# Expert weights in half loads, the residual's buffer lent to one of them, and a regrouped first and last stage

## The reference

```python
x = x + merged @ w_out                                   # x1
h2 = rms_norm(x, norm_ffn)
x = x + moe_ffn(h2, ...)        # 32 experts, each token goes to 2 of them:
#   y = (silu(xb @ w_gate[e]) * (xb @ w_up[e])) @ w_down[e], weighted and added
gate = sigmoid(rms_norm(x, norm_ple) @ w_ple_gate)
x = x + gate * (pemb @ w_ple_proj)                       # pemb: 320 rows of 256
y = rms_norm(x, final_norm)
```

## Time and profile before

| | |
|---|---|
| median of 3 runs | 1094.8 us (1091.55 to 1095.89) |
| the profiled execution | 1092.05 us, its span 1090.4 us |
| PE matmul busy | 1051.1 us (96%) |
| PE weight load busy | 539.3 us (49%) |
| DVE, ACT, POOL busy | 26%, 21%, 9% |
| mean granted TensorE clock | 0.983 |
| chain that ended last: PE, DMA | 50%, 10% |
| expert gate and up loads, issue to landing | 20.6 to 26.0 us (medians) |

### The profile page before, as it was taken

How to read it: one execution, slowest core, us unless ns; L and a number is a source line. 1 busy time by engine, 2 the same in 40 slices (tenths; PEclk the granted TensorE clock), 3 DMA queues, 4 the chain that set the end, 5 groups by cost and what they waited for, 6 DMA issues and landing times.

```text
span 1090.4 us, 14358 instructions
## 1 busy us (share of the span) xinstructions
PE 1051.1 (96%) x5786; PEld 539.3 (49%) x5786; DVE 285.7 (26%) x771; ACT 232.6 (21%) x488; POOL 98.7 (9%) x142
## 2 busy tenths in 40 slices
PE   6999999999999999999989999999999999999994
PEld 3468887555666667775533333333333333333342
DVE  1122011466334324111441111111111111122513
ACT  2012011266322244000221111111111111111333
POOL 0020031000222220000020000000000000001000
PEclk8999999999999999999979999999999999999997
DMA  9972239220545578563349999999999999999801
GB/s 329 263 248 40 78 85 187 78 78 1 165 147 161 176 291 191 222 229 157 113 161 386 426 427 428 426 428 427 427 428 429 428 427 428 425 429 421 266 1 49
DMA packets 57251, 286.32 MB, mean 263 GB/s; under 512 B 10273, under 2 KB 14650, under 8 KB 44844
## 3 DMA queue, kind: packets, MB, share of 16 engines
q1 hardware_dynamic: 47020, 256.99, 60.9%
q0 software_dynamic: 9936, 28.46, 9.0%
q10 hardware_dynamic: 240, 0.09, 0.0%
HBM read 276.57 MB, written 18.25 MB: 270 GB/s over the span
## 4 chain that ended last, share of the span: by engine, by line
PE 50%; DMA 10%; DVE 1%; issue 1%; ACT 0%; POOL 0%; DVEq 0%; SPq 0%; POOLq 0%; ACTq 0%
PE ps L1119 17%; PE ps L554 9%; PE ps L1143 8%; DMA late<-in_w_exp_up_dram 7%; PE ps L1091 4%; PE ps L1014 3%; PE ps L610 3%; DMA late<-y_rows 3%; PE ps L1104 1%; PE ps L1095 1%; PE ps L1133 1%; DMA y_rows<-reg_xh,slot_row 1%; PE ps L991 1%; PE ps L617 1%; PE ps L575 1%
## 5 line engine op out<-in xcount | busy, mean ns | idle before, releaser
L1119 PE MATMUL ps<-ring,reg_xh 128*64 128x512 f32 x512 | 150.4, 602 | 4.2 <-DMA ring<-in_w_exp_up_dram 2.5
L1119 PE MATMUL ps<-late,reg_xh 128*64 128x512 f32 x336 | 150.3, 601 | 2.0 <-DMA reg_k<-in_w_exp_up_dram 1.2
L1119 PEld LDWEIGHTS ps<-ring,reg_xh 128*64 128x64 f32 x512 | 47.1, 138 | 89.2 <-issue 86.5
L1482 ACT ACTIVATE reg_xh<-ps 64x512 f32<-64x512 f32 x32 | 34.0, 1063 | 229.7 <-PE ps L1119 229.7
L2053 DVE TENSOR_TENSOR reg_xh<-reg_xh,ps 64x512 f32<-64x512 f32 x32 | 22.1, 691 | 225.9 <-ACT reg_xh L1482 225.9
L1119 PE MATMUL ps<-reg_k,reg_xh 128*64 128x512 f32 x176 | 79.6, 606 | 0.0
L833 PE MATMUL ps<-reg_xh,ring 128*128 128x320 f32 x256 | 73.5, 436 | 0.0
L1119 PEld LDWEIGHTS ps<-late,reg_xh 128*64 128x64 f32 x336 | 44.7, 138 | 47.4 <-issue 45.9
L1091 PE MATMUL ps<-reg_xh 128*64 128x512 f32 x256 | 62.3, 607 | 1.1 <-DVE reg_xh L1971 1.1
L2257 POOL DMA_INDIRECT y_rows<-reg_xh,slot_row x29 | 28.3, 975 | 382.5 <-ACT reg_xh L1493 342.3
L554 PE MATMUL ps<-reg_xh,ring 128*128 128x320 f32 x224 | 60.9, 433 | 0.0
(11 more groups left out here) (403 smaller groups left out, 1339.4 us busy)
## 6 DMA issues: line engine op xcount, KB each, us to landing
ring<-in_w_exp_gate_dram SPq DMA_DIRECT2D x21, 2048.0 KB, 21.5
ring<-in_w_in_dram SPq DMA_DIRECT2D x13, 2048.0 KB, 11.1
late<-in_w_exp_gate_dram SPq DMA_DIRECT2D x11, 2048.0 KB, 20.6
reg_k<-in_w_exp_up_dram SPq DMA_DIRECT2D x11, 2048.0 KB, 25.0
ring<-in_w_exp_down_dram SPq DMA_DIRECT2D x11, 2048.0 KB, 25.0
ring<-in_w_exp_up_dram SPq DMA_DIRECT2D x11, 2048.0 KB, 26.0
reg_o<-in_w_exp_down_dram SPq DMA_DIRECT2D x11, 2048.0 KB, 26.1
late<-in_w_exp_up_dram SPq DMA_DIRECT2D x10, 2048.0 KB, 25.6
```

The lines of the kernel that those rows point to most:

```text
L1119: last = pe.matmul(out[64 * part:64 * part + 64, :], xb[:, k, :], ws_[part][:, k, :], start=(k == 0), stop=(k == KT - 1))
L1482: act.activation(sg.rearrange("p (m q) -> p q m", m=4), ps[0:64, 2 + par, :].rearrange("p (q m) -> p q m", m=4), ACT.Silu).then_inc(silu_d ...
```

## The change

- First products: the first `w_in` chunk is loaded in two halves (k 0 to 3, k 4 to 7). PE starts the first kv product when the first half is there, takes each transposed piece as it is evacuated, waits for the second half at k = 4, and waits for the constants only after that product.
- Expert loads: gate and up are loaded in halves of four k (8 KB per partition, 1 MB each), first halves of both, then second halves. PE signals `half_done` after k = 3 and waits there for the second halves; `load_next` loads the first halves on `half_done` and the second ones on `up_done`. Down stays whole.
- Down of expert 1 is no longer loaded into slot 7 ahead of the switch, but after x has been normalised, into x (3072 floats) and `reg_pc` (1024 floats). ACT restores x from `xn2` times the rms during experts 2 and 3 (`rows_back_to_x`).
- `w_ple_proj` goes into slot 7 ahead of the switch, pemb's transposes move in front of the `w_out` products, and pemb @ w_ple_proj is computed between the ranks, the first gather and expert 0, copied by ACT, and written to memory (`pp_rows`, 1.3 MB). SP reads it back behind w_ple_gate. DVE's first copy of `he` waits for those writes.
- Last stage: `projected` is gone from it; the products with w_ple_gate go by (half, tile), with the first one right after tile 0 is transposed; DVE adds the read-back rows of tiles 0 and 1, then the sums of tile 0, and so on; ACT's copies are reordered likewise.
- The wait for the output stores stands behind the end of the block instead of inside it. (The branch for over 64 rows per expert changes too, and isn't taken with these inputs.)

```diff
@@ load of the first chunk, SP
+                if name == ("kv", 0):
+                    sp.dma_start(slots[slot][:, 0:2048]..., src[:, 0:4, :]).then_inc(early_in, 16)
+                    sp.dma_start(slots[slot][:, 2048:4096]..., src[:, 4:8, :]).then_inc(chunk_in[slot], 16)
+                    continue
@@ SP, ahead of the loop
             load_matrix(1, 1)
-            load_matrix(1, 2)
+            filled(sp, ("br", 1, 7))
+            for k in range(2):
+                sp.dma_start(w_proj[k], w_ple_proj[0, 128 * k:128 * k + 128, :]).then_inc(pp_in, 16)
             load_matrix(2, 0)
             load_matrix(2, 1)
             load_matrix(2, 2)
+            sp.wait_ge(blanked, 96)
+            sp.wait_ge(xn_dve, 3)
+            sp.wait_ge(xn_act, 1)
+            down_1 = w_exp_down[0, 1].rearrange("(p m) n -> p (m n)", p=128)
+            sp.dma_start(x[:, :, :].rearrange("p t n -> p (t n)"), down_1[:, 0:3072]).then_inc(early_in, 16)
+            sp.dma_start(spare[3], down_1[:, 3072:4096]).then_inc(early_in, 16)
+            for t in range(2):
+                for c in range(2):
+                    evacuated(sp, ("pp", c, t))
+                sp.dma_start(pp_rows[128 * t:128 * t + 128, :], pp_rows_sb[t]).then_inc(pp_out, 16)
@@ def load_next(e, p)
-                sp.wait_ge(up_done, e - 2)
-                load_weights(e, 0, EXPERT_SLOTS[p][0])
-                load_weights(e, 1, EXPERT_SLOTS[p][1])
+                for part, done in enumerate((half_done, up_done)):
+                    sp.wait_ge(done, e - 2)
+                    for j in range(2):
+                        load_half(e, j, p, part, part)
@@ PE, gate_up
                 for k in range(KT):
                     ...
+                    if between is not None and k == 3:
+                        last.then_inc(half_done, 1)
+                        pe.wait_ge(*between)
@@ PE, ahead of expert 0
+            projected(0, 0)
+            projected(1, 0)
             pe.wait_ge(assigned, 2)
             ...
+            projected(0, 1)
             ...
             gather(sel[0], ps[:, 0, :], sel_ready, 1, gathered)
-            evacuated(pe, "rank")
+            projected(1, 1)
             pe.wait_ge(xg_added, 1)
             turn_rows(xg_ready, 1, xg_turned)
+            projected_sample()
+            for bank in range(1, 6):
+                pe.wait_ge(bank_read[bank], plan["expert loop"][bank])
@@ PE, last stage
-                for t in range(2):
-                    projected(t)
-                    turned_tile(t)
-                gated(0)
-                projected(2)
+                turned_tile(0)
+                gated(0, 0)
+                turned_tile(1)
                 turned_tile(2)
-                gated(1)
-                gated(2)
+                gated(1, 0)
+                gated(0, 1)
+                gated(1, 1)
+                gated(0, 2)
+                gated(1, 2)
```

More of the change, by code:

```diff
@@ L439, in load_matrix @@
                     sp.wait_ge(v_out, 16)
-                load_weights(e, j, slot)
+                if j < 2:
+                    for part in range(2):
+                        load_half(e, j, e, part, j)
+                else:
+                    load_weights(e, j, slot)
             before = {}
@@ L504, in _ @@
             load_down(31, 1)
-            sp.wait_ge(up_done, NE - 2)
-            for k in range(2):
-                sp.dma_start(w_proj[k], w_ple_proj[0, 128 * k:128 * k + 128, :]).then_inc(pp_in, 16)
             for c in range(2):
@@ L515, in _ @@
                 sp.dma_start(w_pg[c], src).then_inc(pg_in[c], 16)
+            for t, (t0, rows) in enumerate(TILES):
+                sp.dma_start(pp[0:rows, t, :], pp_rows[t0:t0 + rows, :]).then_inc(pp_in, 16)
             sp.wait_ge(ranked, 1)
@@ L1000, in _ @@
                         by_channel(("br", j, 4 * c + m), w, m, uT if j == 0 else obT, "mx" if (j, c, m) == (0, 0, 0) else None)
+            pe.wait_ge(p_in_s, 32)
+            for k in range(2):
+                out = begin(("ppT", k))
+                for t, (t0, rows) in enumerate(TILES):
+                    last = pe.transpose(out[:, t0:t0 + rows], p_in[0:rows, t, 128 * k:128 * k + 128], ident[0:rows, 0:rows])
+                finish(last, ("ppT", k))
             def mixed_out(c, t, ks=range(KT)):
@@ L1134, in turn_once, with rows_of, down @@
                 return last
-            def down(w_down, hb, out, rows=(0, 1, 2, 3), sg_count=None):
-                w = w_down.rearrange("p (k n) -> p k n", k=4)
+            def rows_of(slot):
+                return [slots[slot][:, 1024 * m:1024 * m + 1024] for m in range(4)]
+            def down(w, hb, out, rows=(0, 1, 2, 3), sg_count=None):
                 for m in rows:
@@ L1449, in root @@
                 act.activation(stat[:, 2, 2, ts], stat[:, 2, 1, ts], ACT.Sqrt).then_inc(rms_ready, 1)
+            for k in range(2):
+                src = filled(act, ("ppT", k))
+                release(act.activation(pT[:, k, :], src[:, 0:N], ACT.Copy), ("ppT", k))
             load_sqrt(2)
@@ L2077, in _, with main_rows @@
             expert_steps(NE // 2 - 1, 1, True)
-            for t, (_, rows) in enumerate(TILES):
+            def main_rows(t):
+                rows = TILES[t][1]
+                dve.wait_ge(x1_back, (1, 2, 4)[t])
                 dve.wait_ge(rows_back[t], 32)
```

251 lines of the change are left out of this document (160 added, 91 removed).

## The result

The changed kernel takes 1086.7 us (median of 20 runs) against 1092.7 us for the kernel before (20 runs beside it): ratio 0.9941, 95% interval 0.9923 to 0.996. One of the changed kernel's runs took 2737 us; the ratios here leave out such slow runs. By the medians the change is 6.0 us faster, where 14.7 were forecast: inside the range, but far short of the gain. By the mark that the prediction set, 0.5%, it is just faster, and the interval reaches past that mark. The profiled execution took 1089.8 us, 3 us above the median, and has a span of 1088.2 us (before: 1090.4).

The account below looks back on a forecast made before the run. PE was taken to bound the front and last stage, the DMA queue the expert loop's end. Terms -5.5 + 1.7 - 1.3 + 2.0 - 9.6 - 2.0 = -14.7 us gave 1077.4, put at 1078; range 1068 to 1090.

Parts of the forecast that it names:

- First products: Kernel's start: PE starts at about 10.6 us instead of 14.3 on the split load; 5.5 us gained, between 3.7 and 5.9.
- Transposes of pemb: Ahead of the w_out products, where nothing hides them: 1.7 us lost.
- Switch: Ahead of expert 0: five pieces, 8.6 us, partly covered, start it 4.5 us later; its product ends some 2.7 us later.
- Half loads: the start of the queue: Expert loads from expert 3: early first halves leave the DMA queue dry for less time; 1.3 us gained.
- Smaller packets: Gate and up loads in 8 KB runs: up to 4.2 us lost on 29 experts, 2 taken.
- Packets of 8 KB are slow: Rival, gate and up loads: 8 KB packets run at 387 GB/s, + 30 us, 1105 us; chance 0.07.
- Last stage: After the experts, without `projected`: PE ends at 1064.7 instead of 1074.3 us; 9.6 us gained, between 6 and 11.
- The last stage keeps its bound: Rival: last stage gives 6 us or less and the switch costs its slow price, 1084 us; chance 0.14.
- The switch eats the lead: Rival: expert 0 starts so late that first halves are issued no earlier than whole loads; 1090 us, chance 0.11.
- End: Kernel's end: the block's closing runs beside the last store; 0 to 2.8 us saved, 2 taken.
- signs listed: Among them: 427 or 421 GB/s from 600 us, queue never dry after 575 us, line 610 starting at about 1025 us.
- three signs of being wrong: A rate below 420 GB/s, PE waiting at k = 3 in the first twenty experts, or a gap between gated products.

Follow-up runs that it names:

- whole_first: `whole` with the first w_in matrix loaded as one 2 MB load again: 1084.2 us, ratio 0.9909 to the kernel before.
- whole: The changed kernel with gate and up loaded whole again, behind `up_done`: 1079.5 us, ratio 0.9874 to the kernel before.
- last_whole: The changed kernel with gate and up of expert 31 alone loaded whole: 1084.1 us, ratio 0.9912 to the kernel before.
- early_halves: The changed kernel with halves kept only for experts 0 to 3, whole loads from expert 4 on: 1081.6 us, ratio 0.988 to the kernel before.
- halves_one_wait: The changed kernel with an expert's four half loads all issued behind `up_done`: 1086.8 us, ratio 0.9934 to the kernel before.
- whole_extra: `whole` with four further, overwritten products in front of each gated piece of the last stage: 1099.6 us, ratio 1.0056 to the kernel before.
- whole_half_pp: `whole` without half of the projection of pemb at the switch: 1077.3 us, ratio 0.9849 to the kernel before.
- parts64: Whole-load kernel with each gate and up matrix in two loads of 64 partitions, 16 KB runs, behind `up_done`: 1491.0 us, ratio 1.3644 to the kernel before.

## Why the prediction fell short, point by point

- *First products, 5.5 us.* Right: 3.8 to 6.1 us by twelve profiles. The products began at 10.4 to 11.1 us (forecast 10.6) and took 7.14 or up to 8.8 us, by the clock. Each of the twelve is one execution; `whole_first` prices the half load itself at 3.8 us, with an uncertainty of 3.
- *Transposes of pemb, 1.7 us.* They take 1.09 us (499.49 to 500.58 us), less than was said: the 1.81 us before were read where the granted clock was 0.50.
- *Switch.* The forecast put expert 0 up to 1 us behind 557.89 us; `whole` has 558.42, the others with its switch and front 555 to 559 us, and the changed one, with its late front, 559.95. Right. The clock of expert 0's product, which was to be regained, was in some executions and not in others.
- *Half loads: the start of the queue, 1.3 us.* This is one of the two steps that failed, and it is larger than it looks. The 1.3 is a net figure. The switch makes expert 0's product end 2.7 us later, so whole loads would have lost all time up to 573.5 us (580.6 + 2.7 - 9.8), halves up to 569.5: the early give-back was booked with 4.0 us, as if all of it reached the end. The first halves did come early: due at 562.1 us on the clock of the run (565.9 less the lead of 3.8), they are issued at 562.52 in `last_whole`, 561.0 in `early_halves`. But `halves_one_wait`, which gives nothing back early, has the time of the changed kernel, 0.1 us more by the medians, 0.8 less by the ratios, with an uncertainty of 3. In place of 4.0 us stands nothing that can be told from zero. Some profiles show a place where it goes, PE's wait for the table of rows; the rest is open.
- *Smaller packets, 2 us.* This is the step that failed most. The working was sound: a fixed part of 9 ns a packet gave 1.5% on gate and up, 4.2 us. Then, with no row for it, I took 2, about the middle between that and nothing. The rate measured is 423 GB/s, which is 0.9% on all the bytes of the full stretch, some 4 us. And it was priced as if a late queue handed its delay on unchanged. In place of 2 us stand 7.3 by the medians of `halves_one_wait` and `whole` (6.6 by their ratios, 9.1 in their profiles), since the delay meets the end of the queue: PE, which in the kernel before had its down 30 and 31 without waiting, waits 2 to 4 us for each and comes back in part at the lower clock (5.35 us twice in the changed kernel, where 3.65 were needed), and the last load itself takes 4.2 us longer to land. That it is the size of the packets, and not the number of the loads, is not shown.
- Together: the forecast had the half loads 2.0 us better than whole ones (4.0 less 2.0), the medians have them 7.2 us worse. These 9.2 us are the whole of the miss (14.7 forecast, 6.0 measured) and half a microsecond more.
- *The rival "Packets of 8 KB are slow"* was put too far out. It asked for 387 GB/s and 5.5% less rate, and so had 0.07; the 1% that came needed no such case, and the worst value that the bounds gave the packets was 4.2 us.
- *Last stage, 9.6 us.* Right in its mechanism: the gated stretch takes 36.5 us (forecast 36.4) in every kernel with this last stage, but for the two whose first gated product ran in part at the lower clock (38.1 and 38.2) and `whole_extra` with its added work, and there 1 us of PE is 1 us of the whole. From down 31's landing to PE's end it is 60.0 us before, 48.5 in `whole`, 11.5 less.
- *The other rivals.* "The last stage keeps its bound" was wrong: it gave what was forecast. "The switch eats the lead" was wrong in its condition: the first halves are issued at 565.3 us in the changed kernel's profile and at 561.0 to 562.5 in those with the full gain of the front, ahead of 566.72. But the switch's price is real, as what PE gains there arrives at down 31's product (`whole_half_pp`).
- *End, 2 us.* 2.5 us by the traces, 1.7 by the medians.
- *The sum without half loads.* Taking the 1.3 and the 2.0 out would give 15.4 us, but then the switch's 2.7 us count, which only the early give-back hid: -5.5 + 1.7 + 2.7 - 9.6 - 2.0 = -12.7 us. `whole` has 13.0 by the medians, 12.7 by the spans, and issues expert 3's first load at 565.64 us, where 565.6 follow from the forecast (569.4 less 3.8). That the sum agrees so well is in part luck. A lead of 1.1 us was to reach the last stage; `whole` is 2.0 us ahead of before at the issue of down 31 and 1.2 behind at its landing (32.8 against 29.6 us behind the issue). These 2.3 us are missing, and the last stage, counted from that landing, gives 1.9 more than the 9.6 and the end 0.5 more than the 2.0. The 1 MB of w_ple_proj that the forecast took out of the queue there brought nothing to down 31. Why it lands later stays open; it is neither the gain's load nor w_ple_gate.
- Of the signs listed, the rate (423, between the 421 and the 427 that were named) and line 610's counterpart 13 us late were the ones that pointed at the truth. None of the three signs of being wrong came: the windows from 600 us on stayed above 420 GB/s, PE is busy throughout from 600 to 900 us, and there is no gap between the gated products. They looked for larger faults than the one there was.

## What to carry to other kernels

Where the DMA queue is full for hundreds of microseconds, a percent of its rate is a term of its own over all its bytes: take the whole of the estimate that the packet size gives, and weigh it against what cutting the loads can bring, which is at most the time in which the queue would have been dry. Follow a late queue to its last load: what PE had covered before turns into a wait, and the wait can cost again through the clock. Write a gain and the cost that it hides as two terms: the 1.3 us here were a gain of 4.0, of which nothing could be seen at the end, and a cost of 2.7. When cutting a load, keep all 128 partitions in each piece and the runs long.

## What the runs showed of the hardware

- Loads of 64 partitions with runs of 16 KB move 216 to 224 GB/s (`parts64`, windows of 100 us from 600 to 1000 us) with the engines at a share of 1.01, half of the 427 of 128 partitions with the same runs. The Trainium skill, "DMA: Bandwidth & Descriptors", section "The descriptor swizzle", says that partitions 0 to 63 are written through the even ports and 64 to 127 through the odd ones; the trace agrees with a load of half the partitions having half the ports. Its section "Rules for kernel authors" says of two transfers to disjoint partition halves "Don't bother — they serialize"; the trace agrees with that too, since two such loads one after the other, each at half the rate, move 219 GB/s and not 427. The ports themselves are in no view here.
- Late in the loop SP spends up to 6.5 us on an issue of a load in the kernels with halves (over 1.5 us for the first time at 776 us in `halves_one_wait`, at 807 us in the changed kernel), where it is 0.3 to 0.4 us in before and `whole`. Two issues, in the changed kernel and in `whole`:

```profile
957.50 4.21 SPq L441 DMA_DIRECT2D reg_k<-in_w_exp_up_dram  x1
```

```profile
961.46 0.42 SPq L436 DMA_DIRECT2D ring<-in_w_exp_up_dram  x1
```

  The queue ahead is no deeper in bytes in the first (its half loads land 29 to 34 us behind their issue from 930 to 985 us, the loads of `whole` 33 to 40), but it has more packets. In `parts64`, with as many loads as with halves but packets of 16 KB, the issues of gate and up loads take no more than 0.6 us from 1000 to 1330 us. There loads land 52 to 80 us behind their issue at 219 GB/s, so the queue is as deep in bytes. So it seems to go with the packets and not with the number of loads.
- 9200 more packets (67416 against 58199 in `whole`) and twice the number of gate and up loads cost 0.9% of the rate. Spread over the 58 loads that came in addition in the full stretch, the 4 us are 0.07 us for each; the Trainium skill, "DMA: Bandwidth & Descriptors", section "Anatomy of one DMA", gives a DMA that GpSimd issues 2.0 us beside its bytes. The loads here are issued by SP, and no run shows such a cost of loads in a full queue.
- Behind a wait of 3.36 us down 31's product took 6.29 instead of 3.65 us (clock 0.58 in that window), behind one of 1.47 us 3.65. The length of the wait alone doesn't decide it: behind 2.26 and 2.71 us it took 5.35 us in the changed kernel, behind 2.62 us 3.65 in `halves_one_wait` (down 30).
